# Twenty-eight TensorE transposes of a two-block kernel handed to the DMA crossbar, and a second PSUM bank for the attention heads

## The reference

```python
# first block
proj = rms_norm(x) @ w_in                       # a, gate, q, k, v
mix  = concat([conformer_conv(a, gate), neighbourhood_attention(q, k, v)]) @ w_out
x = x + rms_norm(mix)
x = x + rms_norm(square(relu(rms_norm(x) @ w_up)) @ w_down)
# second block
proj = rms_norm_2(x) @ w_in_2                   # q_a k_a v_a o_a i_a f_a z_a c_q c_kv k_r z_b g_a g_b
h_a = rms_norm_2(mlstm(...))
y_a = (sigmoid(o_a) * h_a * silu(z_a)) @ w_a
q_b, k_nope, v_b = from rms_norm_2(c_q) @ w_uq and rms_norm_2(c_kv) @ w_ukv
o_b = causal_attention(q_b, k_b, v_b)           # 16 heads
y_b = (o_b * silu(z_b)) @ w_b
return x + (sigmoid(g_a) * y_a + sigmoid(g_b) * y_b) @ w_out_2
```

## Time and profile before

| | |
|---|---|
| median of three executions | 2162.8 us (2161.03 to 2163.23) |
| profiled execution | 2163.23 us, its span 2161.4 us |
| PE busy | 2148.8 us (99%) |
| DVE busy, ACT busy | 1382.7 us (64%), 1079.9 us (50%) |
| DMA | 198 GB/s over the span |

### The profile page before, as it was taken

One profiled execution on the slowest core, in us unless ns is written; L12 is line 12 of the kernel. 1 busy time (PEld: TensorE's weight loads), 2 busy tenths in 40 slices (PEclk: granted clock), 3 DMA queues, 4 the chain that ended last, 5 costly groups with the idle time before them and its releaser, 6 DMA issues.

```text
span 2161.4 us, 27345 instructions
## 1 busy us (share of the span) xinstructions
PE 2148.8 (99%) x9852; PEld 1777.6 (82%) x9852; DVE 1382.7 (64%) x1862; ACT 1079.9 (50%) x1503; POOL 60.2 (3%) x70
## 2 busy tenths in 40 slices
PE   9999999999999999999999999999999999999999
PEld 7888887888888888888788888888888888888887
DVE  6898857765665656656777445566445666666764
ACT  6544565654444444444575445554444655564442
POOL 1000100000000000000000000000000000000000
PEclk9999999999999999999999999999999999999999
DMA  9665446776766766767565765556666554555875
GB/s 328 183 189 165 145 144 213 211 214 199 234 199 209 214 202 202 212 189 218 165 207 186 222 193 176 176 162 201 201 202 202 177 184 146 175 176 181 323 238 165
DMA packets 152933, 428.29 MB, mean 198 GB/s; under 512 B 48216, under 2 KB 48736, under 8 KB 152544
## 3 DMA queue, kind: packets, MB, share of 16 engines
q1 hardware_dynamic: 150768, 420.64, 62.4%
q0 software_dynamic: 1744, 5.77, 0.8%
q10 hardware_dynamic: 288, 0.14, 0.0%
HBM read 407.60 MB, written 10.49 MB: 193 GB/s over the span
## 4 chain that ended last, share of the span: by engine, by line
PE 96%; DVE 2%; ACT 1%; issue 1%; DMA 0%; POOL 0%; ACTq 0%; DVEq 0%
PE g L594 30%; PE g L596 30%; PE g L595 30%; PE s L573 2%; PE s L651 1%; DVE wlo L1457 1%; PE s L805 0%; PE s L804 0%; DVE arena L1522 0%; DVE ta_lo L1634 0%; PE s L633 0%; PE s L643 0%; PE s L812 0%; PE s L689 0%; ACT whi L907 0%
## 5 line engine op out<-in xcount | busy, mean ns | idle before, releaser
L1457 DVE TENSOR_TENSOR wlo<-raw,whi 128x1024 fp32r<-128x1024 f32 x732 | 891.1, 1222 | 564.1 <-ACT whi L907 561.8
L907 ACT ACTIVATE whi<-raw 128x1024 fp32r<-128x1024 f32 x732 | 771.2, 1058 | 677.3 <-PE g L596 659.7
L594 PE MATMUL g<-whi,ta_hi 128*128 128x512 f32 x1920 | 762.9, 397 | 4.3 <-DVE wlo L1449 2.0
L596 PE MATMUL g<-whi,ta_lo 128*128 128x512 f32 x1920 | 749.3, 390 | 0.0
L595 PE MATMUL g<-wlo,ta_hi 128*128 128x512 f32 x1920 | 748.0, 390 | 0.0
L594 PEld LDWEIGHTS g<-whi,ta_hi 128*128 128x128 f32 x1920 | 360.9, 188 | 79.8 <-issue 6.0
L596 PEld LDWEIGHTS g<-whi,ta_lo 128*128 128x128 f32 x1920 | 360.8, 188 | 77.2
L595 PEld LDWEIGHTS g<-wlo,ta_hi 128*128 128x128 f32 x1920 | 361.4, 188 | 72.2
L594 PE MATMUL g<-whi,tb_hi 128*128 128x512 f32 x1008 | 397.8, 395 | 0.2 <-ACT arena L1096 0.2
L596 PE MATMUL g<-whi,tb_lo 128*128 128x512 f32 x1008 | 393.0, 390 | 0.0
L595 PE MATMUL g<-wlo,tb_hi 128*128 128x512 f32 x1008 | 392.6, 389 | 0.0
(11 more groups left out here) (226 smaller groups left out, 975.1 us busy)
## 6 DMA issues: line engine op xcount, KB each, us to landing
raw<-in_w_in SPq DMA_DIRECT2D x318, 512.0 KB, 4.1
raw<-in_w_up SPq DMA_DIRECT2D x128, 512.0 KB, 4.1
raw<-in_w_down SPq DMA_DIRECT2D x128, 512.0 KB, 4.1
raw<-in_w_out SPq DMA_DIRECT2D x64, 512.0 KB, 4.2
raw<-in_w_a SPq DMA_DIRECT2D x32, 512.0 KB, 4.2
raw<-in_w_b SPq DMA_DIRECT2D x32, 512.0 KB, 4.7
raw<-in_w_ukv SPq DMA_DIRECT2D x16, 512.0 KB, 4.3
raw<-in_w_uq SPq DMA_DIRECT2D x12, 512.0 KB, 3.6
```

The lines of the kernel that those rows point to most:

```text
L594: e.matmul(o, xh, wh, start=first, stop=False)
L596: ins = e.matmul(o, xl, wh, start=False, stop=last)
L907: e.activation(whi[u % RING][:, 0:n], raw[u % RAW][:, 0:n], ACT.Copy).then_inc(s_hi, 1)
L1457: e.tensor_tensor(l, r, h.bitcast(F32), ALU.subtract).then_inc(s_lo, 1)
```

## The change

All four kinds, `ml`, `lat`, `ao` and `yt`, take the crossbar path of the `up` results; 28 calls of `turn` leave PE's program. For each of the 14 new jobs DVE gets two cut copies and two join copies (`cut_words`, `join_words`), and SP four DMA transposes. The writing of high and low part stays on ACT and DVE and reads SBUF instead of PSUM. The table `CBM` gives each job its three buffers. The new slots: for `ml` the cut 5, transposes 8, join 11 and high part 12 slots behind `ML0` of the pair's second head; for `lat` cut E + 1, transposes E + 4, join E + 8, high part E + 9; for `ao` see `AO_T` (cut, transposes, high part, with the join one slot ahead of it); for `yt` cut E + 1, transposes E + 3, join E + 7, high and low part E + 8, where E + 8 is also the slot of the next `yb1` stripe's sum. The attention heads put probabilities and output into banks 1 and 2 in turn. The turns that remain on PE beside the attention use bank 3 alone; ahead of it they alternate between 2 and 3 as before. The second `uqr` turn moves from E + 12 to E + 16. The rest of the diff renames semaphores and adds waits for buffers that have new users.

```diff
-        PL = ar(14576, 1024).bitcast(I16).rearrange("p (h t n) -> p h t n", h=2, t=2)
-        PT = ar(15600, 1024).bitcast(I16).rearrange("p (h c n) -> p h c n", h=2, c=4)
-        UZ = ar(16624, 1024)
+        def planes(v):
+            return v.bitcast(I16).rearrange("p (h t n) -> p h t n", h=2, t=2)
+
+        def turned(v):
+            return v.bitcast(I16).rearrange("p (h c n) -> p h c n", h=2, c=4)
+
+        def chunks(v, pair):
+            return v[:, 512 * pair:512 * pair + 512].rearrange("p (k n) -> p k n", k=2)
...
+        flat = [b[:, :] for b in STG] + [ar(15360, 1024)]
+        CBM = {}
+        for i in range(16):
+            CBM["up", i] = (ar(14576, 1024), ar(15600, 1024), ar(16624, 1024))
+        for n in range(4):
+            CBM["ml", n] = (ar(13360, 1024), flat[n % 2], ar(14384, 1024))
+        for w in range(2):
+            CBM["lat", w] = (ar(16384, 1024), ar(17408, 1024), ar(16384, 1024))
+        for n in range(4):
+            b = (flat[3], flat[4], flat[4], ar(10240, 1024))[n]
+            CBM["ao", n] = (b, ar(13312 + 1024 * (n % 2), 1024), b)
+        for n in range(4):
+            CBM["yt", n] = tuple(ar(4096 + 3072 * (n % 2) + 1024 * m, 1024) for m in range(3))
+        CBN = {job: i for i, job in enumerate(CBM)}
+        joined = [job for job in CBM if CBM[job][2] is not None]
+
+        def cut(job):
+
+            return 2 * CBN[job] + 2
...
+        ML_T = (8, 11, 12)
+
+        AO_T = ((-1, 1, 6), (-1, 1, 6), (1, 3, 17), (-1, 2, 7))
...
-        use += [(AO0[k // 2] + 2 * (k % 2), "ao", k) for k in range(8)]
-        TBK = {(name, k): 2 + i % 2 for i, (_, name, k) in enumerate(sorted(use))}
+
+
+        TBK = {(name, k): 3 if slot >= AT0[0] else 2 + i % 2 for i, (slot, name, k) in enumerate(sorted(use))}
...
-                        b = bank(1, (at_c, i + 1))
+                        b = bank(1 + i % 2, (at_c, i + 1))
...
-            def y_side():
-                for n in range(4):
-                    for pair in range(2):
-                        yield E(f"yb1{n}") + 3 + pair
-                        k = 2 * n + pair
-                        b = bank(k % 4, (yt_h, k + 1), (yt_l, k + 1))
-                        q.wait_ge(yb_s, n + 5)
-                        turn(b, SG[2 + n % 2], pair).then_inc(yt_t.sem, 1)
...
             def y_side():
                 for n in range(4):
+                    yield E(f"yb1{n}") + 8
+                    q.wait_ge(w_join, join_of(("yt", n)))
+                    q.wait_ge(s_mm, mm_of("gb3"))
                     for pair in range(2):
-                        yield E(f"yb1{n}") + 3 + pair
-                        k = 2 * n + pair
-                        q.wait_ge(yt_t, k + 1)
-                        q.wait_ge(s_mm, mm_of("gb3"))
-                        turn_hi(ta_hi, 4 * n + 2 * pair, k % 4, 0.5).then_inc(yt_h.sem, 1)
+                        kt = 4 * n + 2 * pair
+                        e.activation(ta_hi[:, kt:kt + 2, :], chunks(CBM["yt", n][2], pair), ACT.Copy, scale=0.5).then_inc(
+                            yt_h.sem, 1)
...
+            def cut_words(job, src):
+
+                for h in range(2):
+                    e.tensor_copy(planes(CBM[job][0])[:, h], words(src)[:, h].rearrange("p (t n) -> p t n", t=2)).then_inc(
+                        w_cut.sem, 1)
+
+            def join_words(job):
+
+                q.wait_ge(d_turn, 64 * CBN[job] + 64)
+                for h in range(2):
+                    e.tensor_copy(words(CBM[job][2])[:, h].rearrange("p (c n) -> p c n", c=4),
+                                  turned(CBM[job][1])[:, h]).then_inc(w_join.sem, 1)
...
+                            yield E(st.name) + 1
+                            q.wait_ge(yb_s, k + 1)
+                            q.wait_ge(at_x, 16)
+                            q.wait_ge(d_turn, 64 * CBN["yt", n])
+                            cut_words(("yt", n), flat[2 + n % 2])
+                            yield E(st.name) + 7
+                            q.wait_ge(yt_h, 2 * n - 2)
+                            q.wait_ge(yt_l, 2 * n - 2)
+                            join_words(("yt", n))
+                            yield E(st.name) + 8
                             for pair in range(2):
-                                yield E(st.name) + 3 + pair
                                 i = 2 * n + pair
                                 q.wait_ge(yt_h, i + 1)
-                                e.scalar_tensor_tensor(ta_lo[:, 2 * i:2 * i + 2, :], two(i % 4), 0.5,
+                                q.wait_ge(w_join, join_of(("yt", n)))
+                                e.scalar_tensor_tensor(ta_lo[:, 2 * i:2 * i + 2, :], chunks(CBM["yt", n][2], pair), 0.5,
...
-                for i in range(16):
-                    yield E(f"up{i // 2}{i % 2}") + 4
-                    q.wait_ge(up_p, 2 * i + 2)
-                    q.wait_ge(up_w, 2 * i)
+                for job, j in CBN.items():
+                    name, n = job
+                    if name == "up":
+                        yield E(f"up{n // 2}{n % 2}") + 4
+                    elif name == "qk2":
+                        yield E(f"qk2{n}") + 4
+                    elif name == "ml":
+                        yield ML0[2 * n + 1] + ML_T[0]
+                    elif name == "lat":
+                        yield E(("cq", "ckv")[n]) + 4
+                        q.wait_ge(lat_q, 2 * n + 2)
+                    elif name == "ao":
+                        yield AO0[n] + AO_T[n][1]
+                    else:
+                        yield E(f"yb1{n}") + 3
+                    q.wait_ge(d_turn, 64 * j)
+                    q.wait_ge(w_cut, cut(job))
+                    if name in ("up", "lat", "yt") and n > 0:
+                        q.wait_ge(w_join, join_of((name, n - 1)))
+                    to, src = turned(CBM[job][1]), planes(CBM[job][0])
                     for h in range(2):
                         for t in range(2):
-                            e.dma_start_transpose(PT[:, h, :, t * P:(t + 1) * P], PL[:, h, t]).then_inc(d_turn.sem, 16)
+                            e.dma_start_transpose(to[:, h, :, t * P:(t + 1) * P], src[:, h, t]).then_inc(d_turn.sem, 16)
```

More of the change, by code:

```diff
@@ L540, in two_blocks @@
         use += [(E(f"qk2{k // 2}") + 2 + 4 * (k % 2), "qk2", k) for k in range(8)]
[L541 to L542 removed]
+        use += [(E(f"uqr{k // 2}") + (12, 16)[k // 2] + 2 * (k % 2), "qr", k) for k in range(4)]
         use += [(E(f"uqn{k // 4}{k // 2 % 2}") + 2 + 2 * (k % 2), "uq", k) for k in range(8)]
@@ L728, in ml_side @@
                         parts += [(ML0[h], "s", h), (ML0[h] + 4, "o", h)]
-                    parts += [(ML0[2 * n + 1] + 8 + 2 * pair, "t", pair) for pair in range(2)]
                     for slot, part, h in sorted(parts):
@@ L747, in ml_side @@
                             e.matmul(b2[:, 0:258], s[:, 256:384], v[:, 1], start=False, stop=True).then_inc(ml_o, 1)
-                        else:
-                            b = bank(h, (ml_h, 2 * n + h + 1), (ml_l, 2 * n + h + 1))
-                            q.wait_ge(ml_x, 2 * n + 2)
-                            turn(b, SG[n % 2], h).then_inc(ml_t, 1)
-            def lat_side():
-                for w, name in enumerate(("cq", "ckv")):
-                    for pair in range(2):
-                        yield E(name) + 1 + pair
-                        b = bank(TBK["lat", 2 * w + pair], (lat_h, 2 * w + pair + 1), (lat_l, 2 * w + pair + 1))
-                        q.wait_ge(lat_e, w + 1)
-                        turn(b, SG[w], pair).then_inc(lat_t.sem, 1)
             def uqr_side():
@@ L1227, in ml_side @@
                         parts += [(ML0[h], "e", h), (ML0[h] + 4, "q", h)]
-                    parts += [(ML0[2 * n + 1] + 8 + 2 * pair, "t", pair) for pair in range(2)]
+                    parts += [(ML0[2 * n + 1] + ML_T[2], "t", pair) for pair in range(2)]
                     for slot, part, h in sorted(parts):
@@ L1281, in zb_side @@
                     if n == 0:
-                        q.wait_ge(lat_t, 4)
+                        q.wait_ge(w_cut, cut(("lat", 1)))
                         q.wait_ge(lat_q, 4)
@@ L1870, in ml_side @@
                         parts += [(ML0[h], "a", h), (ML0[h], "s", h), (ML0[h] + 4, "x", h), (ML0[h] + 4, "y", h)]
-                    parts += [(ML0[2 * n + 1] + 8 + 2 * pair, "t", pair) for pair in range(2)]
+                    parts += [(ML0[2 * n + 1] + 5, "u", n), (ML0[2 * n + 1] + ML_T[1], "v", n)]
+                    parts += [(ML0[2 * n + 1] + ML_T[2] + 1, "w", pair) for pair in range(2)]
                     for slot, part, h in sorted(parts):
@@ L2293, in out_side @@
             def out_side():
-                after = ((kr_t, 4), (yb_s, 7), (yb_s, 8), (yt_t, 6))
+                after = ((ao_l, 8), (yb_s, 7), (yb_s, 8), (w_cut, cut(("yt", 2))))
                 for n in range(4):
```

160 lines of the change are left out of this document (89 added, 71 removed).

## The result

| | before | after |
|---|---|---|
| median | 2162.0 us (2161.03 to 2163.23, 4 executions) | 2176.97 us (2175.98 to 2178.20, 4 executions) |
| ratio, 95% interval | | 1.0069 (1.0052 to 1.0087) |
| span of the profiled execution | 2161.4 us | 2175.3 us |

The account below looks back on a forecast made before the run. PE's queue was taken as the bound. From the profiled 2163.2 us: -13.4 turns, +15.7 wait in the last stripes, +1.7 clock, +0.5 attention and banks = 2167.7; less 0.4 for the median, 2167.3 us, range 2154 to 2175.

Parts of the forecast that it names:

- Turns: On PE: 28 turns at 0.48 us each leave its queue and nothing takes their place, -13.4 us.
- The chain of the last stripes: Last four stripes: each round is one serial chain DVE, SP, crossbar, DVE, ACT, DVE; PE waits 15.7 us around `out0`.
- the clock: PE in `out0`: a slow spell behind the wait ahead of k tile 12, +1.7 us, bounds 0 and 3.4.
- L = 6.4: Crossbar path: all four transposes have landed 6.4 us after SP begins them; bounds 6.1 to 7.6.
- `ml`, priced at 0: `ml` jobs: joins wait some 1 to 3 us for the transposes, but this is covered, so costs 0.
- the ring: Weight buffers: a weight's low part may be 8.6 us late; DVE's delay stays under that and is made up.
- Attention and banks: Attention stretch: 0.1 us for bank 3 alone, 0 for alternating banks, 0.4 us at head 7's softmax; together 0.5 us.
- The rule of the Trainium skill: Crossbar path: transposes are as fast as regular DMAs, which would make the whole 6.8 us shorter.
- L = 4.7: Last stripes, rival: transposes land as fast as a 512 KB load, in 4.7 us; wait 8.9, time 2160.5 us; chance 4%.
- The rival of hidden turning: Last stripes: turning is hidden as in the `up` stage, so the change gains its turns; 2149.9 us, chance 15%.

Follow-up runs that it names:

- e10_plain_copy: Changed kernel with the four transposes of each `yt` job replaced by plain transfers of the same size: 2173.51 us, ratio to before 1.0055.
- e2_yt_late: Changed kernel with `yt` joins and low parts three slots later (the last one slot), transposes waiting for the join two jobs back: 2163.87 us, ratio to before 1.0011.
- e8_yt_late2: e2_yt_late with each `yt` cut waiting for one job less of landed transposes, and the transposes one slot earlier: 2158.54 us, ratio to before 0.9985.
- e3_ml_late: Changed kernel with joins, high parts and low parts of all four `ml` jobs three slots later: 2172.12 us, ratio to before 1.0051.
- e4_ao1_late: Changed kernel with the join, high part and low part of the second `ao` job three slots later: 2172.63 us, ratio to before 1.0049.
- e7_banks_only: Kernel before the change, with only the attention heads in banks 1 and 2 and other turns of that stretch in bank 3: 2162.27 us, ratio 1.0002.
- e9_best: Changed kernel with the reorderings of e3_ml_late, e4_ao1_late and e8_yt_late2 together: 2149.67 us, ratio to before 0.9943.

## Why the prediction was off, point by point

The prediction said 2167.3 us, the kernel takes 2177.0 us. Against the profiled execution before, it summed to +4.5 us. The pairs show +13.9, and +15.2 without the lucky 1.3 us ahead of the change's places. The 10.7 us between +4.5 and +15.2 are 4.5 us at `ml`, 5.1 at `ao` and 2.0 in the last stripes, less 1.0 that the turns gained more.

- **Turns, -13.4 us: right.** They measure -14.4, with the order of two rotary turns in it (2.62 us between slots 1164 and 1270, where four turns at 0.48 us are 1.9).
- **The chain of the last stripes, +15.7 and +1.7 for the clock: right in mechanism, 2.0 us too small.** 19.4 us were lost. I said that the first pair of `yb13` is ready 64.6 us after the first sum starts. Its low part ran from 2098.81 to 2099.5, with the first sum at 2032.99: 66.5 us. The mis-sized term is L = 6.4. It was the case of most `up` jobs, and here it is 6.93 in the mean, because two of four jobs have one issue of SP stretched to 6.1 us in all, as in the earlier trace rows. 4 times 0.53 is 2.1 us. `e10_plain_copy` shows about that factor again with another L, and `e2_yt_late` and `e8_yt_late2` show that the order makes the chain: there the same transposes cost 5.9 and 1.9 us where they cost 19.4. The clock was counted behind one wait and fell behind three. The spell behind the last wait cost 1.5 us by the pairs (12.39 at slot 1416, 13.92 at 1420), close to the 1.7 priced; the two before it lie ahead of a later wait, which they shorten. That they cost nothing more is argued from this and was not tested.
- **`ml`, priced at 0: wrong, 4.5 us.** The step that failed is "DVE's delay stays under the 8.6 us of the ring and is made up before the next". The delay did stay within the ring (4.95 and 2.72 us, 7.7 together). But I held it only against the weights and the next job, and not against the job's own consumer: the fourth job feeds k tile 12 of `ya0`, six slots (8.2 us) behind its low part. Two sizes were off as well. The join waited 5 us and not 1 to 3 (the four `ml` joins 17.3 us in all): I counted the slots between transposes and join, but DVE had run ahead of them and stood from 1480.7 on. And I counted DVE's wait alone, where ACT stands at the high part at the same time, so that DVE waits once more behind its join. `e3_ml_late` shows that the order makes the loss: three slots later, the same jobs cost 0.3 us (-5.83 at slot 1020, -5.54 at 1028).
- **Attention and banks, 0.5 us: wrong, 5.6 us.** I looked for the stall at the first `ao` job, on DVE, in front of head 7's softmax. It is at the second, on ACT, in front of the copy of `uqn10`, and behind it comes a slow clock. "The copies of `ao` lie beside weights in the same way" is the failed step: ACT has more than weights behind that high part. `e4_ao1_late` shows it: with that high part three slots later, 5.6 us become 1.5. That alternating the banks gains nothing was right (`e7_banks_only`).
- **The rule of the Trainium skill** (Advanced Engine Details and Errata, X-Bar Transpose (TRN2): transposes are as fast as regular DMAs) was set against rows of a 512 KB load. The like of it is `e10_plain_copy`. By their landing the rule agrees (3.3 against 3.5 us), by the queue's time it does not (1.26 against 0.59 us an issue). From the first issue to the join the four plain transfers take 5.8 us in the mean and the transposes 6.9. So L = 4.7, the price of that rival, was too low even for plain transfers: it was read off one load, and four transfers take four issues.
- **The rival of hidden turning** (2149.9 us, if DVE reached the next sum without the join) is wrong for the order that was made. It is what `e9_best` does, at 2149.7 us. That the two figures agree within 0.2 us is in part luck: the rival gains 12.9 us from 2162.8, `e9_best` gains 12.0 from 2161.65, and it still has a stall of 1.4 us at the second `ao` job.

So nearly all that was missed lies in one kind of place: a DMA round trip was called covered by the ring of weights, and neither the other results queued behind the waiting engines nor the second engine in the trip was looked at.

## What to carry to other kernels

When work is handed from the bounding engine to a DMA round trip, list for every engine that takes part what is queued behind its wait (weights, other results, the trip's own last step) and when each is needed; two in-order engines that wait for each other wait twice. Put the receiving end of the trip as late as its consumer allows, behind the next piece of work of each of them: the same 56 DMA transposes made this kernel 15 us slower with the joins early and 12 us faster with most of them one to three slots later (for `yt` with the transposes a slot earlier and two semaphore waits loosened as well). And do not move the transposes ahead of a load that is needed first, since it then waits for all four of them.
